# A gated recurrence cut into four units, and the scan beside it split over two engines

## The reference, cut to what matters

```python
r  = sigmoid(einsum('blhi,hij->blhj', xh, wa) + ba)
ig = sigmoid(einsum('blhi,hij->blhj', xh, wx) + bx)
log_a = -8.0 * r * softplus(-lam)
a = exp(log_a)
bterm = sqrt(-expm1(2.0 * log_a)) * (ig * xf)
# h[t] = a[t] * h[t-1] + bterm[t]
```

## Time and profile before

| what | us |
|---|---|
| median of three runs (3225.57 to 3227.97) | 3226.82 |
| the profiled execution | 3228.15 |
| its span from the first to the last instruction | 3226.6 |
| TensorE busy in the span | 2741.6 (85%) |
| VectorE busy | 1507.3 (47%) |
| GpSimd busy | 1124.5 (35%) |
| ScalarE busy | 753.1 (23%) |

### The profile page before, as it was taken

The page is one execution under the profiler, slowest core; times in us unless marked ns, Lnnn a source line. Parts: engine busy times, 40 slices in busy tenths (PEclk is TensorE's granted clock), DMA queues, the critical chain, the costliest instruction groups (busy, mean ns, idle before and its releaser), DMA issues.

```text
span 3226.6 us, 36649 instructions
## 1 busy us (share of the span) xinstructions
PE 2741.6 (85%) x13087; PEld 2113.6 (66%) x13087; DVE 1507.3 (47%) x1800; ACT 753.1 (23%) x904; POOL 1124.5 (35%) x1187
## 2 busy tenths in 40 slices
PE   7993556988987699698998899999299999997998
PEld 6652344544543577587885678877298878886777
DVE  2207996354454322144232755555755545555411
ACT  1210222224234011222111311111332323232111
POOL 0002986888888300001110443332142424332000
PEclk8796777998998799799998999999599999998999
DMA  4410222010110466624113223332212121313332
GB/s 150 168 65 30 65 74 75 27 49 20 42 42 13 159 202 200 175 73 179 40 33 69 98 100 118 120 127 98 90 45 89 60 102 53 108 37 118 107 102 66
DMA packets 256395, 289.27 MB, mean 90 GB/s; under 512 B 34688, under 2 KB 222376, under 8 KB 255920
## 3 DMA queue, kind: packets, MB, share of 16 engines
q1 hardware_dynamic: 200800, 198.36, 19.6%
q10 hardware_dynamic: 50672, 72.89, 6.3%
q0 software_dynamic: 4832, 16.78, 1.6%
HBM read 194.70 MB, written 93.29 MB: 89 GB/s over the span
## 4 chain that ended last, share of the span: by engine, by line
PE 63%; DVE 13%; POOL 11%; issue 7%; ACT 2%; DMA 1%; ACTq 1%; POOLq 1%; SPq 1%; DVEq 0%
PE ps L130 54%; PE ps L1097 6%; POOL s_scan_tmp L2251 4%; POOL s_scan_tmp L2249 3%; POOL arena L2254 3%; DVE arena L1712 1%; PE ps L961 1%; PE ps L955 1%; DVE arena L1694 1%; DVE arena L1691 1%; DVE xc_part L2006 1%; DVE arena L1690 1%; DVE arena L1689 1%; DVE arena L1688 1%; DVE norm_tmp L1567 1%
## 5 line engine op out<-in xcount | busy, mean ns | idle before, releaser
L130 PE MATMUL ps<-arena,weights 128*128 128x512 f32 (+2 forms) x2432 | 761.3, 502 | 77.7 <-ACT arena L1225 64.6
L130 PEld LDWEIGHTS ps<-arena,weights 128*128 128x128 f32 (+1 forms) x2432 | 403.8, 180 | 423.7 <-issue 322.8
L130 PE MATMUL ps<-h_part,in_weight_parts 128*128 128x512 f32 (+1 forms) x1920 | 407.9, 373 | 13.8 <-DVE h_part L1556 7.6
L130 PEld LDWEIGHTS ps<-h_part,in_weight_parts 128*128 128x128 f32 x1920 | 334.7, 189 | 81.9 <-DVE h_part L1556 9.6
L130 PE MATMUL ps<-v_part,p_part 128*128 128x512 f32 x1248 | 299.4, 399 | 0.1
L130 PEld LDWEIGHTS ps<-v_part,p_part 128*128 128x128 f32 x1248 | 237.4, 192 | 50.3 <-issue 0.9
L130 PE MATMUL ps<-q_part,xc_part 128*128 128x256 f32 x1920 | 249.7, 290 | 12.6 <-DVE q_part L2039 10.6
L130 PEld LDWEIGHTS ps<-q_part,xc_part 128*128 128x128 f32 x1920 | 239.5, 196 | 13.9 <-DVE q_part L2039 11.3
L1097 PE MATMUL ps<-wo_part,mx_part 128*128 128x512 f32 x768 | 180.8, 397 | 14.1 <-DVE mx_part L2006 8.6
L2311 POOL TENSOR_TENSOR in_weight_parts<-weights,ones 128x1024 fp32r<-128x1024 f32 x32 | 77.5, 2422 | 305.2 <-PE ps L130 231.5
L1097 PEld LDWEIGHTS ps<-wo_part,mx_part 128*128 128x128 f32 x768 | 146.5, 192 | 45.1 <-issue 8.7
(11 more groups left out here) (342 smaller groups left out, 3970.6 us busy)
## 6 DMA issues: line engine op xcount, KB each, us to landing
weights<-in_e_w_in SPq DMA_DIRECT2D x32, 512.0 KB, 4.3
weights<-in_o_w_in SPq DMA_DIRECT2D x32, 512.0 KB, 4.4
arena<-in_mod_w POOLq DMA_DIRECT2D x30, 512.0 KB, 5.6
s_out_maps<-arena ACTq DMA_DIRECT2D x16, 640.0 KB, 2.9
arena<-s_out_maps SPq DMA_DIRECT2D x16, 640.0 KB, 4.5
ml_xcv<-arena ACTq DMA_DIRECT2D x16, 640.0 KB, 5.2
xm_tiles<-ml_xm SPq DMA_DIRECT2D x16, 640.0 KB, 3.8
xc_full<-ml_xcv SPq DMA_DIRECT2D x4, 2560.0 KB, 10.2
```

What stands on the lines that cost most here:

```text
L130: return nc.tensor.matmul(o, lhsT, rhs, start=(k == 0), stop=(k == n - 1))
```

## The change

The recurrence's gated part goes by units u = 0 to 3 (direction d = u // 2, half s = u % 2) and not by directions with both halves. Of a unit, gate a now uses accumulator 0 and gate x accumulator 1. ScalarE does the root of unit u - 1 between the sigmoids of unit u and its exponential. VectorE's order is gated(0), then gated(u) and recurrence(u - 1) for u = 1 to 3, then recurrence(3). ScalarE's units 2 and 3 wait for the scans of units 0 and 1.

The S5 scan is split by groups: GpSimd keeps groups 0 to 31 (all 160 steps, at 128 x 64), VectorE takes groups 32 to 63. Its 160 steps are set into the four iterations, 40 in each: 4 and 2 ahead of the convolutions, 10 ahead of the products with `SG`, and 3 at the start and 3 at the end of each gated(u). The scratch is split likewise. What follows the stage waits for both halves.

TensorE:

```diff
-                for d in range(2):
+                for u in range(4):
+                    d, s = u // 2, u % 2
                     for m in range(2):
-                        for s in range(2):
-                            pe.wait_ge(*past(f"rg_ev{s}", 6 * i + 2 + 2 * d + m))
+                        pe.wait_ge(*past(f"rg_ev{m}", 6 * i + (2 + u)))
...
-                            last.then_inc(sem(f"rg_gmm{s}"), 1)
+                        last.then_inc(sem(f"rg_gmm{m}"), 1)
```

ScalarE (the lines taken out are those of the loop over d in point 4):

```diff
+                def root(u):
+                    act.wait_ge(*past("rg_om", 4 * i + (u + 1)))
+                    nc.scalar.activation(RT[:, u % 2], RT[:, u % 2], ACT.Sqrt).then_inc(sem("rg_sq"), 1)
+
+                for u in range(4):
+                    d, s = u // 2, u % 2
+                    if u >= 2:
+                        act.wait_ge(*past("rg_dir", 4 * i + (u - 1)))
                     for m, (dst, c0) in enumerate(((RT, C_BA), (IT, C_BX))):
+                        act.wait_ge(*past(f"rg_gmm{m}", 4 * i + (u + 1)))
+                        nc.scalar.activation(dst[:, s], ps3[m], ACT.Sigmoid, bias=PV[:, bass.ds(2 * i + (c0 + 8 * d + s), 1)]).then_inc(sem(f"rg_ev{m}"), 1)
+                    if u:
+                        root(u - 1)
+                    act.wait_ge(*past("rg_ev0", 6 * i + (3 + u)))
+                    nc.scalar.activation(AT[:, s], RT[:, s], ACT.Exp, scale=lamc[:, bass.ds(2 * i + (8 * d + s), 1)]).then_inc(sem("rg_at"), 1)
+                    act.wait_ge(*past("rg_at", 8 * i + (2 * u + 1)))
+                    nc.scalar.activation(RT[:, s], RT[:, s], ACT.Tanh, scale=lamc[:, bass.ds(2 * i + (16 + 8 * d + s), 1)]).then_inc(sem("rg_at"), 1)
+                root(3)
```

VectorE:

```diff
+                def scan_steps(n):
+
+                    for j in range(step[0], step[0] + n):
+                        z = WZ[:, bass.ds(SH * i + j, 1), :, HG:G].rearrange("p j r g -> p (j r) g")
+                        w = WZ[:, bass.ds(SH * i + (j + 1), 1), :, HG:G].rearrange("p j r g -> p (j r) g")
+                        dve.wait_ge(*past("scan_v", 4 * SH * i + (4 * j + 1)))
+                        V.tensor_tensor(s1, z, A1h, ALU.mult).then_inc(sem("scan_v"), 1)
+                        V.tensor_tensor(s2[:, ::-1], z, A2h, ALU.mult).then_inc(sem("scan_v"), 1)
+                        dve.wait_ge(*past("scan_v", 4 * SH * i + (4 * j + 3)))
+                        V.tensor_tensor(s1, s1, s2, ALU.add).then_inc(sem("scan_v"), 1)
+                        dve.wait_ge(*past("scan_v", 4 * SH * i + (4 * j + 4)))
+                        V.tensor_tensor(w, w, s1, ALU.add).then_inc(sem("scan_v"), 1)
+                    step[0] += n
...
+                def gated(u):
+
+                    s = u % 2
+                    scan_steps(3)
+                    dve.wait_ge(*past("rg_ev1", 6 * i + (3 + u)))
+                    ilink(V.tensor_tensor(IT[:, s], IT[:, s], xcb[:, s], ALU.mult))
+                    if u:
+                        dve.wait_ge(*past("rg_om", 4 * i + u))
+                    dve.wait_ge(*past("rg_at", 8 * i + (2 * u + 2)))
+                    ilink(V.tensor_tensor(TT[:, 0:TOK], AT[:, s], AT[:, s], ALU.mult))
+                    V.scalar_tensor_tensor(out=RT[:, s], in0=TT[:, 0:TOK], scalar=1.0, in1=RT[:, s], op0=ALU.add, op1=ALU.mult).then_inc(sem("rg_om"), 1)
+                    scan_steps(3)
+
+                def recurrence(u):
+
+                    d, s = u // 2, u % 2
+                    dve.wait_ge(*past("rg_sq", 4 * i + (u + 1)))
...
+                    ilink(V.tensor_tensor(IT[:, s], IT[:, s], RT[:, s], ALU.mult))
...
+                gated(0)
+                for u in range(1, 4):
+                    gated(u)
+                    recurrence(u - 1)
+                recurrence(3)
```

More of the change, by code:

```diff
@@ L245, in build @@
         scanP = sb("s5_scan_tmp", 256)
-        SP1 = scanP[:, 0:128].rearrange("p (r g) -> p r g", r=2)
-        SP2 = scanP[:, 128:256].rearrange("p (r g) -> p r g", r=2)
+        SH, HG = NJ // RH, G // 2
+        SPs = [[scanP[:, 128 * h + 64 * v:128 * h + 64 * v + 64].rearrange("p (r g) -> p r g", r=2) for v in range(2)] for h in range(2)]
         nat = rb(14336, 1280).rearrange("p (v q) -> p v q", q=64)
@@ L1730, in _ @@
             dve.wait_ge(*past("e_mm1", NB // 2))
-            n0, per = link_n[0], 17
+            dve.wait_ge(*past("wz_a", NB))
+            dve.wait_ge(*past("wz_v", NB))
+            dve.wait_ge(*past("lam_ready", 1))
+            V.memset(WZ[:, 0, :, HG:G], 0.0).then_inc(sem("scan_v"), 1)
+            A1h, A2h = A1[:, :, HG:G], A2[:, :, HG:G]
+            s1, s2 = SPs[1]
+            n0, per = link_n[0], 23
             with dve.Fori(0, RH) as i:
-                k = [0]
+                k, step = [0], [0]
                 def ilink(ins):
@@ L1775, in _ @@
+                def recurrence(u):
+                    d, s = u // 2, u % 2
+                    dve.wait_ge(*past("rg_sq", 4 * i + (u + 1)))
+                    if u == 0:
+                        dve.wait_ge(*past("bo_stored", 16 * i))
+                    ilink(V.tensor_tensor(IT[:, s], IT[:, s], RT[:, s], ALU.mult))
                     if d == 0:
-                        dve.wait_ge(*past("bo_stored", 16 * i))
-                        for s in range(2):
-                            last = V.tensor_tensor_scan(HH[:, s], AT[:, s], IT[:, s], 0.0, ALU.mult, ALU.add)
@@ L1795, in _ @@
-                assert k[0] == per, k
+                        V.tensor_tensor_scan(HH[:, s], AT[:, s], IT[:, s], 0.0, ALU.mult, ALU.add).then_inc(sem("rg_dir"), 1)
+                    else:
+                        a, v, o = (z[:, s, 0:CTX][:, ::-1] for z in (AT, IT, RT))
+                        ilink(V.tensor_tensor_scan(o, a, v, 0.0, ALU.mult, ALU.add))
+                        a, v, o = (z[:, s, CTX:TOK][:, ::-1] for z in (AT, IT, RT))
+                        ilink(V.tensor_tensor_scan(o, a, v, RT[:, s, 0:1], ALU.mult, ALU.add))
+                        V.tensor_tensor(HH[:, s], HH[:, s], RT[:, s], ALU.add).then_inc(sem("rg_dir"), 1)
+                        dve.wait_ge(*past("rg_dir", 4 * i + (3 + s)))
+                        V.tensor_tensor(HH[:, s], HH[:, s], SG[:, s], ALU.mult).then_inc(sem("rg_bo"), 1)
@@ L1796, in _ @@
+                gated(0)
[3 more added lines that the diff above has]
+                recurrence(3)
+                assert k[0] == per and step[0] == SH, (k, step)
             link_n[0] = n0 + per * RH
             dve.wait_ge(*past("bo_stored", 16 * RH))
-            dve.wait_ge(*past("scan", 4 * NJ))
+            dve.wait_ge(*past("scan", 4 * NJ + 1))
+            dve.wait_ge(*past("scan_v", 4 * NJ + 1))
             with dve.Fori(0, NB // 2) as i:
```

80 lines of the change are left out of this document (20 added, 60 removed).

## The result

The changed kernel takes 3264.94 us (median of 4 runs, 3262.35 to 3267.96) against 3226.2 of the kernel before on the same chips: ratio 1.0123, interval 1.0105 to 1.014. It is 38.7 us slower; the forecast was +50, its range +24 to +99. The profiled execution took 3267.19 (span 3265.7).

A forecast was written before the change was run, and what follows sets the result against it. TensorE's products led the chain, with GpSimd's scan ending the stage just behind the recurrence loop. Iterations +49.5 and tail +2.9, less 1.8 between branches, gave +50.6 on 3228.15: 3278.8, as run median 3277 us; range 3250 to 3326.

The forecast's parts named there:

- the 1.8 us between the branches: End of the stage: recurrence with store ends at 1065.6, scan at 1067.5; taking the scan off gains at most 1.8 us.
- A step on VectorE: One scan step at 64 columns on VectorE beside GpSimd: 1.25 us taken, between 0.92 and 2.1.
- Alternation: Rival: each VectorE scan instruction waits for a whole one of GpSimd, 2.1 us a step; +127, 3354 us; chance 0.09.
- the known stop: TensorE's wait before the last two gate products, 15.67 us in the kernel before; forecast to stay at 15 us.
- The new stop: TensorE idle at the next iteration's first tile, waiting for unit 3's first sigmoid: 10.5 us.
- The tail: From the tile's release to the last recurrence: 31.3 us instead of 28.4, +2.9; hidden in the first three iterations.
- the walk: One iteration followed in time through the engines' queues: first iteration 131.9 us, 9.9 longer; the three others 13.2 longer each.
- The clock after the new stop: TensorE's lower granted clock after its added wait at the next iteration's first tile: 3.3 us charged.
- the rival with steps of 0.92 us: The same path with VectorE scan steps at their lower end, 0.92 us: +37, 3264 us; no separate chance given.
- GpSimd's scan: GpSimd's 160 steps at half width: 440 us at least, against 526 before; most likely done before the recurrence.
- The price of the new order: Order by units with scan steps costing 0 us: +12, 3239 us; as a rival, chance 0.03.
- the other side: Rival: TensorE's stop at the gates goes if unit 0's scan is done by 92; 3152 us; chance 0.05.

The follow-up runs named there:

- units only: The changed kernel's order by units without VectorE's scan steps; GpSimd does the whole scan at 128x128: 3238.02 us, ratio 1.0035 to the kernel before.
- without GpSimd's half: The changed kernel with GpSimd's scan loop left out, so groups 0 to 31 aren't scanned: 3257.93 us, ratio 1.0096 to the kernel before.
- the exchange of two calls: recurrence(u - 1) put ahead of gated(u): in the changed kernel 3215.26 us; with the whole scan on GpSimd and no VectorE steps 3211.59 us.
- split only: Scan split as in the change, but the old order by directions with both halves: 3267.11 us, ratio 1.0115 to the kernel before.
- hidden steps: The changed kernel with recurrence(u - 1) ahead of gated(u) and the 40 steps placed where VectorE waited: 3172.95 us, ratio 0.9825 to the kernel before.

## Why the prediction was right, point by point

**The bound.** Right: with the scan off the path nothing was left to gain but the 1.8 us between the branches; all else came from the loop.

**A step on VectorE.** 1.25 us taken, 1.24 in the mean measured beside GpSimd and 1.05 alone. The parts: 0.92 from short rows plus gaps for computed addresses was 1.16; measured alone it is 1.05, since only one of the two gaps is there (0.17 ahead of L1762, none ahead of L1757). Contention took 0.2, not 0.1. The two misses cancel. GpSimd's 64-column instruction was estimated at 0.32 and has a median of 0.318. Alternation, 2.1 us, didn't come. By the Trainium skill ("SBUF — State Buffer", section "SBUF: two separate sides") whichever of the two engines starts first holds the shared ports for its whole instruction and the other blocks. On GpSimd's side the trace agrees: L2281 took up to 2.7 us beside a scan of 2.8. On VectorE's side it showed far less than a full block: its short instructions lost 0.05 us on average, 0.13 where one met an instruction of GpSimd's of 0.32.

**No gain at the known stop.** Right: 14.6 us, forecast 15. **The new stop.** Right: 10.2 us, forecast 10.5. The tail stays hidden in the first three iterations, as forecast: there TensorE never waits for ScalarE's copies.

**What was too large.** Forecast +52.4 for the branch, measured +42.0. By pieces: the first iteration took 132.6 where the walk has 131.9, the second 133.1 and the third 132.5 where it has 135.2, the fourth 130.9 (947.70 to 1078.6, the end of the sigmoid that frees the tile) instead of 135.2, and the tail from there 29.2 instead of 31.3. Two terms were mis-sized. The clock after the new stop was charged 3.3 us. I had read that from the first tile behind one of the four stops of the kernel before; the windows behind all four give losses of 1.7 to 3.0. Behind the new stop they give 2.1, 2.0 and 2.4, together 3.4 less than was charged. The other term is VectorE's long instructions, for which 1.65 (the root's product of a unit) and 2.9 (its scan) were taken, twice on the path. They took 1.48 to 1.61 and 2.82. GpSimd's narrower instructions are the reason: in units only, with the same long instructions on VectorE and GpSimd at 128 columns, the medians are 1.74 and 2.96, and without GpSimd's half 1.48 and 2.82. In the last iteration GpSimd had ended, so that the steps were shorter as well.

**A coincidence.** The measured 3264.94 is also what the rival with steps of 0.92 us gave (3264). The steps took 1.24, so that agreement is chance.

**GpSimd's scan.** Wrong as a bound: at least 440 us were forecast, measured were 387 (545.9 to 933.0). I had let the whole delay by VectorE stay as it was and taken off only the width. But the delay goes with the iterations that the scan runs beside. An undisturbed step took 2.33 us at full width and 1.84 at half (medians of their spacing), so 160 of them take 373 and 294 by estimate, and the delays are 153 us over 4.3 iterations and 93 over 2.9: 36 and 32 an iteration. The end of the stage wasn't touched by that, only the last iteration.

**Behind the branch.** -1.8 was forecast, -3.2 came; the weight DMA took 6.7 us instead of 8.35 when GpSimd issued it together with SyncE's loads (6.4 to 6.9 in all eight kernels here in which the store ends the stage, and 5.3 in the one where it came 40 us after those loads). That wasn't foreseen and isn't explained.

**The price of the new order.** +12 forecast, +11 measured. This was the sharpest of the numbers, since it comes from the walk alone. By its profile the branch took 12.7 more, where 14.2 were forecast, and what is behind it 3.2 less, where 1.8 were: +9.5, against +11 by the medians. For the other side I named 92 as the time by which the scan of unit 0 would have to be done, and said that the order gives 101.9 at best. That is so in this order; the exchange of two calls gets nearly there: 2.9 us are left of the stop at the gates with the steps, 3.1 without.

## What to carry to other kernels

Work given to a second engine costs by where it stands in that engine's queue, not by how busy the engine is: in one and the same order the 160 steps cost 29 us of the branch where the change has them and nothing measurable once they were moved (529.0 without steps, 558.4, and 526.6 moved). Before splitting a job over two engines, walk one iteration in time, and put the steps only in front of waits that end on another engine. When a loop is cut into finer units, issue the part that others wait for as soon as its inputs are there: finer units with the next gated part still ahead of the scan made two stops out of one.

## What the runs showed of the hardware

The length of a stop of TensorE doesn't tell what clock follows. Behind four stops of 15.7 us in the kernel before, the granted clock was 0.50, 0.50, 0.58 and 0.50 in the first 4 us and 0.98, 0.76, 1.00 and 0.81 in the next 4. Behind 14.6 us in the changed kernel it was 0.50 and then 0.83, behind 10.2 us 0.50 and then 0.99, behind 22.3 us (split only) 0.50 and then 0.99. A short stop can cost clock too. In the kernel with hidden steps these are the 4 us behind two stops of the same 2.78 us:

```profile
758.63:762.63 4.00, 4.00 (x11) 2.04 (x12) 3.53 (x10) 3.95 (x4) 3.04 (x7) 1.00 0.00 0
979.33:983.33 4.00, 4.00 (x6) 1.70 (x7) 3.39 (x11) 3.95 (x4) 0.00 (x0) 0.57 0.00 0
```

So two stops can lose more to the clock than one: in units only the products took 431.5 us for 425.1 before. With hidden steps, where all stops of the stretch together are 18.8 us and none is over 2.8, they took 423.4.

VectorE's linked 64-column instructions lose 0.2 us a step of four to GpSimd's, while GpSimd's 160 steps take 387 us beside VectorE where undisturbed ones would take some 294 (an estimate, 160 times 1.84). GpSimd's 64-column instruction takes 0.318 us in the median and up to 2.8 beside a scan of 2.8 on VectorE.
